# Pooling layer: the transposes of u and of the gated product made by DMAs on 16-bit halves, with the output projection moved behind both u products

## The chip, the cores and the metric

The kernel runs on one core of a Trainium2 chip. The metric is the device time of one execution in microseconds; lower is better. Five engines work side by side: TensorE (PE), VectorE (DVE), ScalarE (ACT), GpSimd (POOL) and SyncE (SP); 16 DMA engines move data between HBM and the on-chip memory SBUF.

## The reference, cut to what matters

All arithmetic is float32. Two layers (retention, then pooling) each add a branch to the residual `h` of 256 tokens by 2048 columns; the change touches only the pooling layer.

```python
def pool_branch(xn, w_in, w_group, scale, w_out):      # xn (1, 256, 2048)
    u, g = jnp.split(xn @ w_in, 2, axis=-1)            # each 4096 wide
    csum = jnp.cumsum(u.astype(jnp.float32), axis=1)
    outs = []
    for gi, w in enumerate((2, 4, 8, 16)):             # 4 groups of 1024 columns
        lo, hi = gi * 1024, (gi + 1) * 1024
        c_g = csum[..., lo:hi]
        c_lag = jnp.pad(c_g, ((0, 0), (w, 0), (0, 0)))[:, :256]
        cnt = jnp.minimum(t + 1, w)[None, :, None]
        outs.append((c_g - c_lag) / cnt - u32[..., lo:hi])
    d = jnp.stack(outs, axis=2)
    mixed = jnp.einsum('bsgc,gce->bsge', d, w_group).reshape(b, s, 4096) * scale
    return (mixed * jax.nn.silu(g)) @ w_out
```

## The kernel before, in words

**Weights and units.** All weights are streamed once, in the order in which they are used, as `stream`: pieces of 1 MB that SP loads into one of four slots of `w_raw`. A piece holds two units. A unit is two blocks of 128 by 512 weights; in the kernel's 552 units every product is done. float32 products are made of three fp32r products: ACT copies the unit to `w_hi` (`split_hi`, line 615, rounded to fp32r), DVE makes `w_lo = w_raw - w_hi` (`split_lo`, line 878), and PE does hi·hi, hi·lo, lo·hi for two blocks and two token tiles, 12 matmuls of 512 columns per unit (`products`, lines 344 to 346). `w_hi` and `w_lo` are rings of `RING = 4` units: `split_hi` of unit u waits until PE has finished unit u - 4.

**Orders.** Each of PE, ACT and DVE runs an order written out by hand: a loop over the units u of a stage, and behind a named unit some other work ("at u = 6"). So a step of ACT "at u" comes behind `split_hi(u)` and in front of `split_hi(u + 1)`, while PE itself is some units behind. The products go to three pairs of PSUM accumulators A, B and C; the transposes on PE go to two further banks, `side`.

**The pooling layer.** It is `group` for g = 0 to 3 (the first written out, the later three a loop) and then `close(1)`. A group of 1024 columns has two column halves of 512. In a later group PE does, in 56 units:

- u 0 to 7: the u product of the first half into A. Behind unit 3 it transposes the gated product `gm` of the second half of the previous group (`m_transposes(n2 - 1, 1)`).
- u 8 to 23: the output projection of the previous group, four column blocks of 4 units into B, C, A, B. Behind unit 13 it transposes `u` of the first half (`u_transposes(n2)`).
- u 24 to 31: the u product of the second half into C. u 32 to 39: the first gate product into A; behind its fourth unit the transposes of `u` of the second half. u 40 to 47: the second gate product into B.
- u 48 to 51 and 52 to 55: the two group products (`w_group`) into C and B; behind unit 53 the transposes of the first half of this group's `gm`.

The first group has no output projection (40 units). One set of transposes is `transpose4` (line 360): 8 float32 transposes of 128 by 128 against the identity `idn`. Around it, ACT copies the product to `u` (`u_part`, line 701), PE transposes it to `side`, ACT copies it to `uT` (`uT_part`, line 709), DVE does six window steps on it, one per unit (`window_step`, lines 1033 to 1047), and ACT and DVE split the result into `dT_hi` and `dT_lo` (lines 715 and 1053). For the gated product, ACT and DVE read `side` and write `oT_hi` and `oT_lo` for the output projection (`m_hi_part`, line 727; `m_lo_part`, line 1075). DVE adds each block of the projection to `h` (line 1145). `close(1)` starts with 4 units of the embedding projection (A, C, A, C; `emb_out` copies them to `emb`), transposes the last half of `gm` behind its unit 2, and goes on with the last output projection.

## Time and profile before

| | us |
|---|---|
| median of 3 runs (1590.47 to 1590.62) | 1590.62 |
| the profiled execution's own time | 1590.46 |
| its span, first to last instruction | 1588.7 |
| outside the span (1590.46 - 1588.7) | 1.8 |
| PE busy | 1576.0 |
| DVE busy | 1020.1 |
| ACT busy | 734.2 |

The profile is one execution. Busy time counts an engine's computing instructions, not its waits and not its issuing of DMAs. TensorE's mean granted clock is 0.998 of full speed.

### The profile page before, as it was taken

How to read it: one execution, taken by the hardware profiler on the slowest of the kernel's cores; microseconds unless marked ns; L12 is line 12 of the kernel's file. 1: busy time of each engine (PE TensorE's matmuls, PEld its weight loads, DVE VectorE, ACT ScalarE, POOL GpSimd, SP SyncE). 2: the span in 40 equal slices, each digit the busy share in tenths (PEclk: the TensorE clock that was granted, in tenths of full speed). 3: DMA queues.
4: the chain of work that ended last, by engine and by line, in shares of the span. 5: the costliest groups of instructions: out<-in, count | busy, mean ns of one | idle time of the engine just before them, and what ended most of it. 6: DMA issues, size and time to landing. Idle time of an engine off the chain costs nothing.

```text
span 1588.7 us, 19508 instructions
## 1 busy us (share of the span) xinstructions
PE 1576.0 (99%) x7162; PEld 1306.5 (82%) x7162; DVE 1020.1 (64%) x1247; ACT 734.2 (46%) x904; POOL 4.6 (0%) x12
## 2 busy tenths in 40 slices
PE   9999999999999999999999999999999999999997
PEld 6888888888888888888888888888888888888885
DVE  6775666667576666657756665756575657566665
ACT  6444444444443434445645544444444444445553
POOL 0000000000000000000000000000000000000000
PEclk9999999999999999999999999999999999999999
DMA  9555455545545454555455454555555555555551
GB/s 375 211 212 178 166 185 185 185 162 208 185 158 186 183 186 173 197 183 183 163 197 194 179 208 172 201 184 189 184 186 189 204 185 185 185 211 186 185 186 79
DMA packets 43446, 300.04 MB, mean 189 GB/s; under 512 B 4832, under 2 KB 4848, under 8 KB 7824
## 3 DMA queue, kind: packets, MB, share of 16 engines
q1 hardware_dynamic: 42272, 295.45, 51.3%
q0 software_dynamic: 704, 3.27, 0.5%
q10 hardware_dynamic: 432, 0.79, 0.2%
q8 instruction: 26, 0.43, 0.1%
q14 instruction: 12, 0.10, 0.0%
HBM read 297.40 MB, written 2.10 MB: 189 GB/s over the span
## 4 chain that ended last, share of the span: by engine, by line
PE 98%; DVE 1%; DMA 0%; ACT 0%; issue 0%; SPq 0%; DVEq 0%; ACTq 0%
PE accB L344 11%; PE accB L346 11%; PE accB L345 11%; PE accA L346 10%; PE accA L344 10%; PE accA L345 10%; PE accC L344 10%; PE accC L346 10%; PE accC L345 10%; PE side L360 2%; DMA w_raw<-in_stream_dram 0%; PE side L399 0%; PE side L398 0%; PE side L397 0%; PE side L388 0%; PE side L389 0%
## 5 line engine op out<-in xcount | busy, mean ns | idle before, releaser
L878 DVE TENSOR_TENSOR w_lo<-w_raw,w_hi 128x1024 fp32r<-128x1024 f32 x551 | 668.9, 1223 | 388.3 <-ACT w_hi L615 384.1
L615 ACT CAST w_hi<-w_raw 128x1024 fp32r<-128x1024 f32 x551 | 579.3, 1055 | 612.5 <-PE accB L346 253.5
L344 PE MATMUL accA<-w_hi,xa_hi 128*128 128x512 f32 x508 | 198.9, 392 | 0.0
L346 PE MATMUL accA<-w_hi,xa_lo 128*128 128x512 f32 x508 | 197.7, 389 | 0.0
L345 PE MATMUL accA<-w_lo,xa_hi 128*128 128x512 f32 x508 | 197.7, 389 | 0.0
L344 PE MATMUL accC<-w_hi,xa_hi 128*128 128x512 f32 x384 | 150.7, 392 | 0.6 <-DVE w_lo L878 0.6
L346 PE MATMUL accC<-w_hi,xa_lo 128*128 128x512 f32 x384 | 149.5, 389 | 0.0
L345 PE MATMUL accC<-w_lo,xa_hi 128*128 128x512 f32 x384 | 149.4, 389 | 0.0
L344 PE MATMUL accB<-w_hi,xa_hi 128*128 128x512 f32 x384 | 149.4, 389 | 0.0
L345 PE MATMUL accB<-w_lo,xa_hi 128*128 128x512 f32 x384 | 149.4, 389 | 0.0
L346 PE MATMUL accB<-w_hi,xa_lo 128*128 128x512 f32 x384 | 149.4, 389 | 0.0
L346 PEld LDWEIGHTS accA<-w_hi,xa_lo 128*128 128x128 f32 x508 | 95.4, 188 | 19.8
L344 PEld LDWEIGHTS accA<-w_hi,xa_hi 128*128 128x128 f32 x508 | 95.4, 188 | 19.3
L345 PEld LDWEIGHTS accA<-w_lo,xa_hi 128*128 128x128 f32 x508 | 95.4, 188 | 19.3
L344 PE MATMUL accB<-w_hi,oT_hi 128*128 128x512 f32 x256 | 99.9, 390 | 0.0
L346 PE MATMUL accB<-w_hi,oT_lo 128*128 128x512 f32 x256 | 99.6, 389 | 0.0
L345 PE MATMUL accB<-w_lo,oT_hi 128*128 128x512 f32 x256 | 99.6, 389 | 0.0
L344 PEld LDWEIGHTS accC<-w_hi,xa_hi 128*128 128x128 f32 x384 | 72.1, 188 | 15.3 <-DVE w_lo L878 1.0
L346 PEld LDWEIGHTS accC<-w_hi,xa_lo 128*128 128x128 f32 x384 | 72.1, 188 | 15.1
L346 PEld LDWEIGHTS accB<-w_hi,xa_lo 128*128 128x128 f32 x384 | 72.1, 188 | 15.0
L345 PEld LDWEIGHTS accB<-w_lo,xa_hi 128*128 128x128 f32 x384 | 72.1, 188 | 14.9
L344 PEld LDWEIGHTS accB<-w_hi,xa_hi 128*128 128x128 f32 x384 | 72.1, 188 | 14.9
(200 smaller groups left out, 2125.0 us busy)
## 6 DMA issues: line engine op xcount, KB each, us to landing
w_raw<-in_stream_dram SPq DMA_DIRECT2D x275, 1024.0 KB, 4.8
h<-in_x_dram SPq DMA_DIRECT2D x4, 512.0 KB, 13.8
xT_raw<-in_xT_dram SPq DMA_DIRECT2D x3, 512.0 KB, 15.4
dec<-in_decay_dram POOLq DMA_DIRECT2D x1, 1024.0 KB, 9.1
fgain<-in_final_gain_dram POOLq DMA_DIRECT2D x1, 1024.0 KB, 5.1
out_dram<-emb SPq DMA_DIRECT2D x1, 1024.0 KB, 3.8
w_raw<-in_stream_dram SPq DMA_DIRECT2D x2, 256.0 KB, 6.4
w_raw<-in_stream_dram SPq DMA_DIRECT2D x1, 512.0 KB, 7.7
```

The source lines that it names most:

```text
L344: pe.matmul(acc[pair][t][:, 0:n], xh, wh, start=first and b == 0, stop=False)
L345: pe.matmul(acc[pair][t][:, 0:n], xh, wl, start=False, stop=False)
L346: mm = pe.matmul(acc[pair][t][:, 0:n], xl, wh, start=False, stop=last and b == UNIT - 1)
L360: mm = pe.transpose(side[j // 2][:, (j % 2) * SEQ + t * P:(j % 2) * SEQ + (t + 1) * P], src(t)[:, tiles + j * P:tiles + (j + 1) * P], idn[:])
L615: act.copy(w_hi[:, r % RING, :], w_raw[:, r // 2, (r % 2) * 1024:(r % 2 + 1) * 1024]).then_inc(hi_ready, 1)
L878: dve.tensor_tensor(w_lo[:, r % RING, :], w_raw[:, r // 2, (r % 2) * 1024:(r % 2 + 1) * 1024], w_hi[:, r % RING, :].bitcast(F32), ALU.subt ...
```

## The change

The float32 tiles `u` and `gm` are transposed without PE. ACT copies a tile of 128 tokens by 512 float32 words, seen as 1024 words of 16 bits, to `halves`, with the lower halves of the words first and the upper halves behind them (`halves_of`, two copies). One unit later ACT issues two DMA transposes of 128 by 1024 16-bit elements (`transpose_halves`). Some units later ACT waits for both to have landed and puts the halves together again, 16 bits beside 16 bits, into `uT` or into `words` (`words_of`, two copies). One such round is a turn: 2 in the first group (u only), 4 in each later one, 14 in all. `halves`, `halvesT` and `words` lie in `emb`, which is not in use until the close. For `gm`, ACT makes `oT_hi` from `words` (`m_words`), and DVE's `m_lo_part` reads `words` where it read `side`. `u_transposes` is gone; `m_transposes` is left only in `close(1)`, for both halves of the last group (behind its units 0 and 2).

In a later group PE's order becomes: u 0 to 7 and 8 to 15 the two u products (A, C), u 16 to 31 the output projection (B, A, C, B), u 32 to 39 and 40 to 47 the gate products (A, C), u 48 to 55 the group products (A, B). The weight stream is put in that order. The turns of ACT in a later group:

| turn | halves | DMA transposes issued | words |
|---|---|---|---|
| `gm`, first half of the previous group | u = 0 | u = 1 | u = 6, with `oT_hi` |
| `gm`, second half of the previous group | u = 6 | u = 7 | u = 13, with `oT_hi` |
| `u`, first half | u = 14 | u = 15 | u = 21 |
| `u`, second half | u = 22 | u = 23 | u = 29 |

In the first group the two turns have halves at u = 11 and 19, the DMAs at 12 and 20, and the words at 18 and 26. The window steps follow the words unit by unit, and the d split comes at six units behind the words. The core of the diff:

```diff
+U_FIRST = (KD_U + 3, 2 * KD_U + 3)
+U_LATER = (2 * KD_U - 2, 3 * KD_U - 2)
+LANDING = 7
+TURNS = 0
...
+        halves = nc.alloc_sbuf_tensor_at("halves", [P, TT, 2, COL], U16, offset=emb0)
+        halvesT = nc.alloc_sbuf_tensor_at("halvesT", [P, 2 * COL // P, SEQ], U16, offset=emb0 + 4096)
+        words = nc.alloc_sbuf_tensor_at("words", [P, COL // P, SEQ], F32, offset=emb0 + 8192)
...
                 if not first:
-                    pe.wait_ge(pg_ready, n2 - 1)
+                    pe.wait_ge(m_ready, n2 - 1)
                 for k in range(KD_U):
                     if first and k % 2 == 0:
                         pe.wait_ge(xT_ready, NC + k // 2 + 1)
                     unit(k, base, "A", xa_hi, xa_lo, k * UNIT, k == 0, k == KD_U - 1, seg)
                     if first and k == 1:
                         h_transposes(2, NC - 1)
-                    if not first and k == 3:
-                        pe.wait_ge(mT_ready, n2 - 1)
-                        m_transposes(n2 - 1, 1)
+                if first:
+                    pe.wait_ge(z_read, NC)
+                else:
+                    pe.wait_ge(pg_ready, n2)
+                for k in range(KD_U):
+                    unit(KD_U + k, base, "C", xa_hi, xa_lo, k * UNIT, k == 0, k == KD_U - 1, seg)
                 if not first:
+                    pe.wait_ge(m_ready, n2)
                     pe.wait_ge(mT_ready, n2)
-                    pe.wait_ge(m_ready, n2)
                     for c in range(NC):
+                        if c == 1:
+                            pe.wait_ge(u_ready, n2 + 1)
                         if c == 2:
-                            pe.wait_ge(u_ready, n2 + 1)
+                            pe.wait_ge(u_ready, n2 + 2)
                         if c == 3:
                             pe.wait_ge(o_read, g * NC + (O_RET + 1))
                         for k in range(PO_U):
-                            unit(KD_U + c * PO_U + k, base, "BCAB"[c], oT_hi, oT_lo, k * UNIT, k == 0,
+                            unit(2 * KD_U + c * PO_U + k, base, "BACB"[c], oT_hi, oT_lo, k * UNIT, k == 0,
                                  k == PO_U - 1, seg)
-                            if c == 1 and k == 1:
-                                u_transposes(n2)
-                    pe.wait_ge(o_read, g * NC + (O_RET + 2))
-                else:
-                    pe.wait_ge(z_read, NC)
-                for k in range(KD_U):
-                    unit(KD_U + o + k, base, "C", xa_hi, xa_lo, k * UNIT, k == 0, k == KD_U - 1, seg)
-                    if first and k == 3:
-                        u_transposes(n2)
                 if first:
                     pe.wait_ge(u_ready, n2 + 1)
                 else:
+                    pe.wait_ge(o_read, g * NC + (O_RET + 2))
+                for k in range(KD_U):
+                    unit(2 * KD_U + o + k, base, "A", xa_hi, xa_lo, k * UNIT, k == 0, k == KD_U - 1, seg)
+                if first:
+                    pe.wait_ge(u_ready, n2 + 2)
+                else:
                     pe.wait_ge(o_read, g * NC + (O_RET + 3))
                 for k in range(KD_U):
-                    unit(2 * KD_U + o + k, base, "A", xa_hi, xa_lo, k * UNIT, k == 0, k == KD_U - 1, seg)
-                    if k == 3:
-                        pe.wait_ge(uT_ready, n2 + 1)
-                        u_transposes(n2 + 1)
+                    unit(3 * KD_U + o + k, base, "C", xa_hi, xa_lo, k * UNIT, k == 0, k == KD_U - 1, seg)
+                pe.wait_ge(d_ready, n2 + 2)
+                pe.wait_ge(pg_ready, n2 + 1)
+                for k in range(PO_U):
+                    unit(4 * KD_U + o + k, base, "A", dT_hi, dT_lo, k * UNIT, k == 0, k == PO_U - 1, seg)
                 if not first:
                     pe.wait_ge(o_read, g * NC + (O_RET + NC))
-                for k in range(KD_U):
-                    unit(3 * KD_U + o + k, base, "B", xa_hi, xa_lo, k * UNIT, k == 0, k == KD_U - 1, seg)
-                pe.wait_ge(d_ready, n2 + 2)
-                pe.wait_ge(u_ready, n2 + 2)
-                for k in range(PO_U):
-                    unit(4 * KD_U + o + k, base, "C", dT_hi, dT_lo, k * UNIT, k == 0, k == PO_U - 1, seg)
-                pe.wait_ge(pg_ready, n2 + 2)
                 for k in range(PO_U):
                     unit(4 * KD_U + PO_U + o + k, base, "B", dT_hi, dT_lo, k * UNIT, k == 0, k == PO_U - 1, seg)
-                    if k == 1:
-                        m_transposes(n2, 0)
...
+                    if c == 0 and layer == 1:
+                        pe.wait_ge(m_ready, 2 * GROUPS - 1)
+                    if c == 1 and layer == 1:
+                        pe.wait_ge(pg_ready, 2 * GROUPS)
                     unit(c, base, "AC"[c % 2], pT_hi[:, layer], pT_lo[:, layer], 0, True, True, seg)
                     if c == 2 and layer == 0:
                         y_transposes(HEADS - 1)
+                    if c == 0 and layer == 1:
+                        m_transposes(2 * GROUPS - 2, 0)
                     if c == 2 and layer == 1:
                         pe.wait_ge(mT_ready, 2 * GROUPS - 1)
                         m_transposes(2 * GROUPS - 1, 1)
...
-            def uT_part(n):
-                act.wait_ge(uT_done, n + 1)
...
+            def u_halves(n):
+                act.wait_ge(u_ready, n + 1)
+                halves_of(u)
+
+            def uT_part(n, turn):
                 if not (isinstance(n, int) and n == 0):
                     act.wait_ge(d_scaled, n)
-                for b in range(2):
-                    cp = act.copy(uT[:, 2 * b:2 * b + 2, :], side[b][:].rearrange("p (k n) -> p k n", n=SEQ))
-                cp.then_inc(uT_ready, 1)
+                words_of(turn, uT)
+
+            def m_halves(n, c):
+                act.wait_ge(m_ready, n + 1)
+                halves_of(gm[:, c, :, :])
+
+            def m_words(n, k0, c, turn):
+                if c:
+                    act.wait_ge(mT_ready, n)
+                words_of(turn, words)
+                act.wait_ge(words_ready, turn * 2 + 2)
+                for j in range(4):
+                    cp = act.activation(oT_hi[:, 4 * c + j, :], words[:, j, :], ACT.Copy, scale=pscale[:, bass.ds(k0 + j, 1)])
+                    if j % 2:
+                        cp.then_inc(mT_hi, 1)
...
+            def halves_of(src):
+
+                for t in range(TT):
+                    act.copy(halves[:, t, :, :], src[:, t, :].bitcast(U16).rearrange("p (n two) -> p two n", two=2)
+                             ).then_inc(halves_ready, 1)
+
+            def transpose_halves():
+
+                for t in range(TT):
+                    act.dma_start_transpose(halvesT[:, :, t * P:(t + 1) * P],
+                                            halves[:, t, :, :].rearrange("p two n -> p (two n)")).then_inc(halvesT_landed, 16)
+
+            def words_of(n, dst):
+
+                act.wait_ge(halvesT_landed, n * (16 * TT) + 16 * TT)
+                for i in range(2):
+                    act.copy(dst[:].bitcast(U16).rearrange("p k (n two) -> p two k n", two=2)[:, i, :, :],
+                             halvesT[:, 4 * i:4 * i + 4, :]).then_inc(words_ready, 1)
...
+                    if not first and u in (1, KD_U - 1):
+                        act.wait_ge(halves_ready, turn * 2 + (2 if u == 1 else 4))
+                    for i, at_u in enumerate(turns):
+                        if u == at_u + 1:
+                            act.wait_ge(halves_ready, turn * 2 + (2 * i + (2 if first else 6)))
                     split_hi(u, base, seg, landings)
+                    if not first and u in (1, KD_U - 1) or u - 1 in turns:
+                        transpose_halves()
...
                     if not first and u == 0:
-                        m_hi_part(n2 - 2, g * KG - KG, 0)
-                    if not first and u == 6:
-                        m_hi_part(n2 - 1, g * KG - KG // 2, 1)
+                        m_halves(n2 - 2, 0)
+                    if not first and u == KD_U - 2:
+                        m_words(n2 - 2, g * KG - KG, 0, turn)
+                        m_halves(n2 - 1, 1)
+                    if not first and u == 2 * KD_U - 3:
+                        m_words(n2 - 1, g * KG - KG // 2, 1, turn + 1)
...
+                    if u == 2 * KD_U + 2:
+                        u_part(n2 + 1, "C", base + 2 * KD_U)
+                    for i, at_u in enumerate(turns):
+                        if u == at_u:
+                            u_halves(n2 + i)
+                        if u == at_u + LANDING:
+                            uT_part(n2 + i, turn + (i if first else i + 2))
+                        if u == at_u + LANDING + WINDOW_STEPS + 1:
+                            d_hi_part(n2 + i, i)
...
-                    if u == 0 and layer == 1:
+                    if u == 3 and layer == 1:
                         m_hi_part(2 * GROUPS - 2, (GROUPS - 1) * KG, 0)
...
-                    if not first and u == 0:
-                        m_lo_part(n2 - 2, g * KG - KG, 0)
                     if not first and u == 2:
                         mix(n2 - 1, 1, "B", base)
-                    if not first and u == 6:
+                    if not first and u == KD_U - 2:
+                        m_lo_part(n2 - 2, g * KG - KG, 0)
+                    if not first and u == 2 * KD_U - 3:
                         m_lo_part(n2 - 1, g * KG - KG // 2, 1)
                     for c in range(NC):
-                        if not first and u == KD_U + PO_U * (c + 1) + 2:
-                            dve.wait_ge(unit_used, base + (KD_U + PO_U * (c + 1)))
+                        if not first and u == 2 * KD_U + PO_U * (c + 1) + 2:
+                            dve.wait_ge(unit_used, base + (2 * KD_U + PO_U * (c + 1)))
                             for t in range(TT):
                                 hc = h[:, t, c * COL:(c + 1) * COL]
-                                ins = dve.tensor_tensor(hc, acc["BCAB"[c]][t][:], hc, ALU.add)
+                                ins = dve.tensor_tensor(hc, acc["BACB"[c]][t][:], hc, ALU.add)
                             ins.then_inc(o_read, 1)
-                    if first and u == early:
-                        dve.wait_ge(inv_landed, 32)
-                    if early <= u <= early + WINDOW_STEPS:
-                        window_step(g, n2, u - early)
-                    if u == early + 6:
-                        d_lo_part(n2, 0)
-                    if 2 * KD_U + o + 6 <= u <= 2 * KD_U + o + 6 + WINDOW_STEPS:
-                        window_step(g, n2 + 1, u - (2 * KD_U + o + 6))
-                    if u == 2 * KD_U + o + 12:
-                        d_lo_part(n2 + 1, 1)
+                    for i, at_u in enumerate(turns):
+                        step = u - at_u - LANDING
+                        if first and i == 0 and step == 0:
+                            dve.wait_ge(inv_landed, 32)
+                        if 0 <= step <= WINDOW_STEPS:
+                            window_step(g, n2 + i, step, turn + (i if first else i + 2))
+                        if step == WINDOW_STEPS + 1:
+                            d_lo_part(n2 + i, i)
...
     for g in range(GROUPS):
         product(pool_in, KD, 0, (g * GDIM, COL))
+        product(pool_in, KD, 0, (g * GDIM + COL, COL))
         if g:
             chunks(pool_out, KG, (g - 1) * KG)
-        product(pool_in, KD, 0, (g * GDIM + COL, COL))
         for c in range(2):
             product(pool_in, KD, 0, (2 * D + g * GDIM + c * COL, COL))
         for c in range(2):
```

## Rows read from the trace of the kernel before

**Rows 1.** The page: the span and the busy times.
```profile
span 1588.7 us, 19508 instructions
PE 1576.0 (99%) x7162; PEld 1306.5 (82%) x7162; DVE 1020.1 (64%) x1247; ACT 734.2 (46%) x904; POOL 4.6 (0%) x12
```

**Rows 2.** The page: the chain that ended last, shares of the span by engine.
```profile
PE 98%; DVE 1%; DMA 0%; ACT 0%; issue 0%; SPq 0%; DVEq 0%; ACTq 0%
```

**Rows 3.** Waits of PE: who waited for whom, us in total, times, longest.
```profile
PE side L588 <- DVE junk L1212: 1.2, 1, 1.2
PE accC L344 <- DVE w_lo L878: 0.6, 1, 0.6
```

**Rows 4.** The chain in order of time: start, us, what; one set a group.
```profile
1063.71 0.87 PE side L360 x8
...
1219.60 0.87 PE side L360 x8
...
1375.49 0.87 PE side L360 x8
```

**Rows 5.** Busy time of one group of 56 units, by engine.
```profile
1063.71:1219.60 155.89, 155.89 (x706) 129.44 (x705) 97.20 (x98) 70.75 (x80) 0.00 (x0) 1.00 0.52 189
```

**Rows 6.** Timeline of PE around one set of transposes: start, us, instruction.
```profile
974.49 0.39 PE L346 MATMUL accA<-w_hi,xa_lo 128*128 128x512 f32 x1
974.72 1.03 PE L360 MATMUL side<-idn,gm 128*128 128x128 f32 x8
...
976.06 0.39 PE L346 MATMUL accA<-w_hi,xa_lo 128*128 128x512 f32 x1
```

**Rows 7.** Groups of instructions by line: count, busy us, mean ns, idle before.
```profile
L615 ACT CAST w_hi<-w_raw 128x1024 fp32r<-128x1024 f32 x551 | 579.3, 1055 | 612.5 <-PE accB L346 253.5 <-PE accA L346 179.4 <-PE accC L346 171.9
...
L1038 DVE SCALAR_TENSOR_TENSOR sums<-sums,wide 128x1024 f32<-128x1024 f32 x24 | 30.7, 1281 | 0.0
...
L627 ACT ACTIVATE junk<-h 128x512 bf16<-128x512 f32 x38 | 23.7, 628 | 17.9 <-DVE h L1022 17.9
...
L709 ACT COPY uT<-side 128x512 f32<-128x512 f32 x16 | 8.6, 590 | 20.2 <-PE side L360 20.2
...
L1145 DVE TENSOR_TENSOR h<-accB,h 128x512 f32<-128x512 f32 x12 | 7.7, 686 | 2.4 <-PE accB L346 2.4
```

**Rows 8.** Timelines of ACT, PE and DVE around one unit's split, PE unhurried.
```profile
964.03 1.06 ACT L615 CAST w_hi<-w_raw 128x1024 fp32r<-128x1024 f32 x1 [1.66 <-PE accB L346]
...
966.56 0.39 PE L344 MATMUL accA<-w_hi,xa_hi 128*128 128x512 f32 x1
...
966.75 1.05 ACT L615 CAST w_hi<-w_raw 128x1024 fp32r<-128x1024 f32 x1 [1.66 <-PE accA L346]
...
967.84 1.23 DVE L878 TENSOR_TENSOR w_lo<-w_raw,w_hi 128x1024 fp32r<-128x1024 f32 x1 [1.38 <-ACT w_hi L615]
```

**Rows 9.** Timeline of ACT around m_hi_part, four activations in one row.
```profile
958.70 1.57 ACT L727 ACTIVATE oT_hi<-side,pscale 128x256 fp32r<-128x256 f32 x4 [2.66 <-PE side L360]
```

**Rows 10.** Timeline of the issuing queues: DMA issues of 256 and 512 KB.
```profile
1.20 0.45 ACTq L823 DMA_DIRECT2D xT_raw<-in_xT_dram  x1
...
12.59 1.93 SPq L278 DMA_DIRECT2D xT_raw<-in_xT_dram  x1
```

**Rows 11.** DMA issues: queue, count, KB each, median us from issue to landing.
```profile
w_raw<-in_stream_dram SPq DMA_DIRECT2D x275, 1024.0 KB, 4.8
...
xT_raw<-in_xT_dram ACTq DMA_DIRECT2D x1, 256.0 KB, 7.0
...
ropes<-in_rope_dram SPq DMA_DIRECT2D x1, 256.0 KB, 15.7
```

**Rows 12.** Waits of ACT for the weight stream: us in total, times, longest.
```profile
ACT w_hi L615 <- DMA w_raw<-in_stream_dram: 6.8, 8, 2.2
```

**Rows 13.** Timeline of ACT in the close, behind PE's transposes.
```profile
1440.75 1.57 ACT L727 ACTIVATE oT_hi<-side,pscale 128x256 fp32r<-128x256 f32 x4 [1.58 <-PE side L360]
1442.20 1.09 ACT L683 COPY emb<-accA 128x512 f32<-128x512 f32 x2
```

More of the change, by code:

```diff
@@ L219, in trunk @@
         st_done = sem("st_done")
+        halves_ready = sem("halves_ready")
+        halvesT_landed = sem("halvesT_landed")
+        words_ready = sem("words_ready")
         pr_whole = sem("pr_whole")
@@ L760, in group @@
                 o = 0 if first else NC * PO_U
-                early = KD_U + (6 if first else PO_U + 4)
                 n2 = g * 2
+                turn = TURNS if first else TURNS - 2 + g * 4
+                turns = U_FIRST if first else U_LATER
                 for u in range(4 * KD_U + 2 * PO_U + o):
+                    if not first and u in (1, KD_U - 1):
[3 more added lines that the diff above has]
+                            act.wait_ge(halves_ready, turn * 2 + (2 * i + (2 if first else 6)))
                     split_hi(u, base, seg, landings)
+                    if not first and u in (1, KD_U - 1) or u - 1 in turns:
+                        transpose_halves()
                     if first and u == 2:
@@ L1023, in add_gated, with window_step @@
                                   ).then_inc(h_ready, 1)
-            def window_step(g, n, i):
+            def window_step(g, n, i, turn):
                 a, b = sums[(i + 1) % 2], sums[i % 2]
@@ L1029, in window_step @@
                 if i == 0:
-                    dve.wait_ge(uT_ready, n + 1)
+                    dve.wait_ge(words_ready, turn * 2 + 2)
                     if not (isinstance(n, int) and n == 0):
@@ L1069, in mix, with m_lo_part @@
                 ins.then_inc(m_ready, 1)
-            def m_lo_part(n, k0, c):
+            def m_lo_part(n, k0, c, last=False):
                 for j in range(4):
@@ L1075, in m_lo_part @@
                     ins = dve.scalar_tensor_tensor(
-                        out=oT_lo[:, 4 * c + j, :], in0=side[j // 2][:, (j % 2) * SEQ:(j % 2 + 1) * SEQ],
+                        out=oT_lo[:, 4 * c + j, :],
+                        in0=side[j // 2][:, (j % 2) * SEQ:(j % 2 + 1) * SEQ] if last else words[:, j, :],
                         scalar=pscale[:, bass.ds(k0 + j, 1)], in1=oT_hi[:, 4 * c + j, :].bitcast(F32),
@@ L1124, in group @@
                 o = 0 if first else NC * PO_U
-                early = KD_U + (6 if first else PO_U + 4)
                 n2 = g * 2
+                turn = TURNS if first else TURNS - 2 + g * 4
+                turns = U_FIRST if first else U_LATER
                 for u in range(4 * KD_U + 2 * PO_U + o):
@@ L1167, in close @@
                     split_lo(u, base, seg)
-                    if u == 0 and layer == 1:
-                        m_lo_part(2 * GROUPS - 2, (GROUPS - 1) * KG, 0)
+                    if u == 3 and layer == 1:
+                        m_lo_part(2 * GROUPS - 2, (GROUPS - 1) * KG, 0, True)
                     if u == 2:
```

27 lines of the change are left out of this document (7 added, 20 removed).

## The prediction

> **What bounds the kernel now.** I read the page's busy times first, then the chain, then who waited for whom, and only then single durations. PE is busy for 1576.0 of 1588.7 us [rows 1], the chain that ended last is 98% PE [rows 2], and PE's own waits in the whole execution are 1.2 and 0.6 us [rows 3]. So time is saved only by taking work from PE's order, and lost only where PE is made to wait. ACT (734.2 us) and DVE (1020.1 us) are far from full [rows 1], but both run in a fixed order in step with PE, so for them a burst at one place counts and not the total.
>
> The unit time comes from ACT's starts, which PE releases: 966.75 - 964.03 = 2.72 us for 12 matmuls, 0.227 each [rows 8]. A later group takes 1219.60 - 1063.71 = 155.89 us, and the next one the same [rows 4]; the stretch is 155.89 us of busy PE, without a gap [rows 5]. 56 units by 2.72 are 152.3; the other 3.6 us are its four sets of transposes.
>
> **What is removed.** Between the matmul at 974.49 and the one at 976.06 lie 1.57 us, in which there would be three steps, 0.68 us, without the transposes [rows 6]. One set so costs PE 0.89 us; 3.6 / 4 gives the same. The chain puts 0.87 us on the eight transposes themselves [rows 4], the rest is the first matmuls behind them. 16 sets exist in the pooling layer, 2 stay in the close, so 14 go: 14 x 0.89 = 12.5 us. This is on the path: PE never waits around them. The matmuls are the same in number and size, so the new order of units saves or costs nothing by itself. A later group should take 152.3 us.
>
> **The accumulators.** The new order must not make PE wait for a pair to be read. Every reader comes two units behind the product's end, and the closest reuse is three: pair B, read at u = 22 of DVE, is needed at u = 28; A, read at 26, at 32; C, read at 30, at 40; the projection waits from u = 16 for `oT`, which DVE has at u = 13. ACT and DVE stand some three units before PE, so each has 8 us or more. Cost 0, covered by these three units; without them it would be one read, 2 x 0.686 us [rows 7], at each change of pair.
>
> **How far ACT may fall behind.** PE starts unit u - 3 at 966.56, ACT starts the split of u at 966.75, DVE ends it at 967.84 + 1.23 = 969.07 [rows 8], and PE needs it at 966.56 + 3 x 2.72 = 974.72. The slack is 5.6 us. ACT's backlog grows at each unit by its work there less 2.72 us. With only a split of 1.06 us [rows 7] it shrinks by 1.66. PE stalls by what the backlog has above 5.6.
>
> **What ACT gets.** A copy of 1024 16-bit elements has no row. The nearest, 1024 float32 elements, takes 1.055 us; two of 512 with a 16-bit output take 2 x 0.628 = 1.26 [rows 7]. If two 16-bit elements went at a time, it would be half of the first, 0.53. I take 1.06, as the engine's time per element is alike in both rows; 1.26 would add 0.2 us per copy, 0.8 at the fullest place. A turn then has halves of 2.1 and words of 2.1 us. For u two copies of 0.590 us go [rows 7]; for `gm` the four activations stay, 1.57 us [rows 9]. ACT's busy time in a group goes from 70.75 [rows 5] to 70.75 + 16 x 1.06 - 4 x 0.59 = 85.3 us, of 152.3.
>
> Let X be the time for which issuing one DMA transpose holds ACT. The bursts of a later group are:
> - u = 0: split and halves, 3.2 us, backlog 0.45. u = 1: split and 2X, backlog 2X - 1.2. PE stalls from X = 3.4 on.
> - u = 6: split, words, activations, halves, 1.06 + 2.1 + 0.2 (a wait for its own copies, estimated) + 1.57 + 2.1 = 7.0, backlog 4.3. u = 7: split and 2X, backlog 2.65 + 2X. PE stalls from X = 1.45 on. This is the tightest place.
> - u = 13 (4.9 us), 14 (3.2), 15: backlog 1.0 + 2X, stalls from X = 2.3.
> - u = 21, 22, 23: backlog 2X - 0.8, stalls from X = 3.2. The two turns of the first group: as u = 0 and 1.
>
> X has no row either. The nearest are plain issues of 256 and 512 KB: 0.45 us on ACT's queue, 1.93 at most on SP's in the crowded start [rows 10]. At 0.45 nothing stalls; at 1.93 the second turn stalls by 2 x (1.93 - 1.45) = 1.0 us, in three groups 2.9 us. I take the nearer one, on ACT's own queue, so 0, and keep 2.9 for the range. Below 0.45 nothing is gained, as PE has no wait left to lose.
>
> **The landing.** Behind the DMAs only ACT waits at first, at the words; but the next splits stand behind it, and DVE's window steps. From issue to words are 13.2 us in the first turn (five units less 0.4), 12.0 in the second, 13.7 and 15.4 in the u turns. Added to the backlogs above, a pair may land up to 14.4, 14.9, about 17.5 and about 19 us behind its issue before PE waits. For 256 KB the rows have 7.0 us on ACT's queue and 15.7 as the worst, in the crowded start [rows 11]. In the steady state 1 MB lands in 4.8 us, so I take under 8 us for the pair: hidden. At 15.7 it costs 1.3 + 0.8 us in each of three groups, 6 us.
>
> The Trainium skill (VectorE: DVE Perf Modes, section "The three transpose paths") speaks against this change: it gives 1309 ns for a 128 by 128 transpose of 16-bit elements by DMA and 390 ns on TensorE. Here eight float32 transposes take 0.87 us, 0.11 each [rows 4]. A turn is 16 such blocks, and by that figure, if they went one by one, 20.9 us; the same skill (Advanced Engine Details and Errata, section "X-Bar Transpose (TRN2)") calls transpose DMAs as fast as regular ones, which would be the 8 us above. No row here shows either.
>
> **The weight stream** gets 14 x 512 KB beside 300 MB. A piece lands in 4.8 us [rows 11], and its slot is asked for about 17.8 us behind its issue (seven units less the split), so 13 us are spare; ACT's waits for it are 6.8 us in all, in 8 waits [rows 12], and PE has none. Cost 0.
>
> **DVE** gets nothing new, but its additions to `h` (2 x 0.686 us) now fall on window steps (1.28 us [rows 7]) at u = 22, 26, 30 and 34. Such a unit is 1.13 + 1.2 + 1.37 = 3.7 us, a plain window unit 2.33. Its backlog stays under some 2.5 us of the 5.6. Cost 0.
>
> **The close.** The set behind unit 0 is new there. ACT makes `oT_hi` from it before it copies the first embedding product out, and PE waits for that copy in front of unit 2. In the same order of ACT now, `oT_hi` starts at 1440.75 and the copies end at 1442.20 + 1.09 = 1443.29 [rows 13], 2.8 us behind the transposes' end at about 1440.47, and PE would be there after 2.8 us. I count 0.2 us.
>
> **The sum**, against the profiled execution: 1590.46 - 12.5 + 0.2 = 1578.2. The median of the runs is 0.16 us above that execution, so 1578.4 us; 0.8% less.
>
> **Rivals.**
> 1. *Partly paid back* (X between 1.45 and 2.9, or copies of 1.26 us, or the second turn landing at 15 to 16 us): the stalls at u = 7 and 15 of the later groups take 1 to 10 us. At X = 2.3 it is 3 x 1.7 = 5.1 us: 1583.5. For it: the fullest unit is 4.3 us behind already. Against: both issue rows are below 2.
> 2. *ACT is held while the DMA transpose runs* (the other side). A transpose can't be one run of bytes; if ACT's queue has to hand it over piece by piece, X grows with its size. The stalls are 3 x [(2X - 2.9) + (2X - 4.6) + (2X - 6.4) + (2X - 6.8)] + 2 x (2X - 6.8), negative terms left out. It decides from X = 2.9, where 3 x (2.9 + 1.2) = 12.3 eat the gain. X = 4 gives 3 x (5.1 + 3.4 + 1.6 + 1.2) + 2.4 = 36 us: 1614. X = 7.0, the landing time of 256 KB [rows 11], gives 3 x (11.1 + 9.4 + 7.6 + 7.2) + 14.4 = 120 us: 1698. Against: plain issues take 0.45 to 1.93 us whatever their size [rows 10].
> 3. *The halves land late* (also slower). It decides from a landing of 16.7 us: 3 x (2.3 + 1.8) = 12.3. At 20 us it is 3 x (5.6 + 5.1 + 2.5 + 1.0) + 2 = 45 us: 1623. For it: 15.7 us occurs for 256 KB [rows 11]. Against: only with many transfers ahead of it. By the Trainium skill's 20.9 us it would be some 55 us more than the forecast.
> 4. *No change* (within 0.2%): stalls that happen to equal the gain, 9 to 15 us.
>
> **Chances.** Forecast 0.48; rival 1 0.13; rival 2 0.21; rival 3 0.12; rival 4 0.06. A measurement of this kernel can tell about 0.2%, 3.2 us, from no change. Faster 0.61, same 0.06, slower 0.33. The likeliest case by itself reaches from 1577.5 to 1584. The range takes in rivals 1 and 4 and the nearer part of 2 and 3: 1576 to 1618, with some 0.18 above it.
>
> **What the profile would show.** PE has 112 transposes fewer; later groups of 152.3 us; ACT some 85 us busy in each; the transposes' issues on ACT's queue below 1.45 us and landed within 13 us; no wait of PE for `w_lo`. Wrong would be: PE waiting for `w_lo` behind u = 7 or 15 (X too small in my sum), ACT waiting for the landing at u = 6 or 13 (rival 3), or waits of ACT for `w_raw` (the stream crowded out).

## The result, and the profile after

| | before | after |
|---|---|---|
| median of 4 runs each, us | 1590.62 | 1579.77 |
| lowest to highest, us | 1590.47 to 1590.75 | 1579.41 to 1579.92 |
| the profiled execution, us | 1590.46 | 1579.41 |
| its span, us | 1588.7 | 1577.6 |

The changed kernel takes 0.9932 of the time, with a 95% interval of 0.9914 to 0.9949: 0.7% faster, 10.9 us. The forecast was 1578.4.

The first lines of the page of the kernel after answer to [rows 1]: PE has 112 instructions and 13.2 us of busy time fewer, ACT 50.9 us more, DVE stays. PE is still busy for 99% of the span.

```profile
span 1577.6 us, 19371 instructions
PE 1562.8 (99%) x7050; PEld 1294.6 (82%) x7050; DVE 1019.1 (65%) x1247; ACT 785.1 (50%) x944; POOL 4.6 (0%) x12
```

The busy time of one later group of 56 units after (columns: the stretch, its length and then PE, PEld, DVE, ACT and POOL) answers to [rows 5]. It is 152.32 us long and PE fills it; the forecast was 152.3. For ACT 85.3 us were forecast, and it has 85.84.

```profile
1109.85:1262.17 152.32, 152.32 (x674) 126.17 (x673) 97.01 (x98) 85.84 (x93) 0.00 (x0) 1.00 0.60 207
```

The waits of PE after (us in total, times, longest) answer to [rows 3]. The waits for `junk` and for `accC` at the start were there before. The one at line 420 belongs to the very first unit, some 8 us into the span. It varies from run to run (0.2 to 1.5 us in the kernels below) and moves nothing behind it: the last transposes of the retention layer start at 857.05 to 857.27 in all these kernels, whatever it is. New in the pooling layer is one wait of 0.8 us for `w_lo`: the sum had none.

```profile
PE side L593 <- DVE junk L1261: 1.2, 1, 1.2
PE accA L420 <- ACT w_hi L656: 1.2, 1, 1.2
PE accA L354 <- DVE w_lo L927: 0.8, 1, 0.8
PE accC L354 <- DVE w_lo L927: 0.7, 1, 0.7
```

It lies in the first group, which I had passed over with the words "as u = 0 and 1". The chain in order of time there (start, us, what) shows ACT from u = 18 to the late split:

```profile
896.22 1.27 ACT u L706 x2
897.49 1.49 ACT uT L753 x2
...
899.79 1.06 ACT w_hi L620
900.84 1.90 ACT halves L740 x2
...
902.76 1.05 ACT w_hi L620
...
904.05 4.17 ACTq L746
...
908.26 1.06 ACT w_hi L620
...
909.34 1.24 DVE w_lo L927
...
910.62 0.50 PE accA L354
```

Two things come together. At u = 18 ACT first copies the second product to `u` and then makes the words of the first turn, so the halves of u = 19 and the issues of u = 20 start from a backlog. And the second of the two issues holds ACT for 4.17 us. The next split starts at 908.26, 5.50 us behind the one before it at 902.76, where 2.72 is the pace. The split of u = 18 had started at 893.55, so at 908.26, three units on, ACT is 908.26 - 893.55 - 8.16 = 6.55 us behind, above the slack of 5.6 by 0.95. The matmul that waited starts 1.23 us behind the one before it (910.62 and 909.39) where 0.23 is the pace, 1.00 late, and the five behind it lose another 0.14: the wait that is listed as 0.84 costs 1.14 us.

The pairs of issues of the first group (two) and of the group behind it (four), from the timeline of ACT (start, us for both issues together):

```profile
878.65 5.60 ACTq L746 DMA_TRANSPOSE halvesT<-halves  x2
902.77 5.45 ACTq L746 DMA_TRANSPOSE halvesT<-halves  x2
957.55 2.79 ACTq L746 DMA_TRANSPOSE halvesT<-halves  x2
978.47 2.77 ACTq L746 DMA_TRANSPOSE halvesT<-halves  x2
998.15 2.62 ACTq L746 DMA_TRANSPOSE halvesT<-halves  x2
1018.03 3.26 ACTq L746 DMA_TRANSPOSE halvesT<-halves  x2
```

So X, which I had taken as 0.45 us, is 1.3 us for one DMA transpose as a rule, and more than that in the two pairs of the first group. SP put out a weight piece just ahead of each of these two:

```profile
878.14 0.33 SPq L294 DMA_DIRECT2D w_raw<-in_stream_dram  x1
...
902.63 0.33 SPq L294 DMA_DIRECT2D w_raw<-in_stream_dram  x1
```

The tightest place of a later group, on ACT's timeline (start, us for all, what, and the idle time ahead with its releaser):

```profile
1123.12 1.05 ACT L620 CAST w_hi<-w_raw 128x1024 fp32r<-128x1024 f32 x1 [1.67 <-PE accA L356]
1124.07 2.57 ACT L753 COPY words<-halvesT 128x1024 uint16<-128x1024 uint16 x2
1126.80 1.71 ACT L728 ACTIVATE oT_hi<-words,pscale 128x256 fp32r<-128x256 f32 x4 [0.15 <-ACT words L753]
1128.41 1.98 ACT L740 COPY halves<-gm 128x1024 uint16<-128x1024 uint16 x2
1130.59 1.05 ACT L620 CAST w_hi<-w_raw 128x1024 fp32r<-128x1024 f32 x1 [0.20 <-ACT halves L740]
1130.60 2.62 ACTq L746 DMA_TRANSPOSE halvesT<-halves  x2
1133.33 2.95 ACT L620 CAST w_hi<-w_raw 128x1024 fp32r<-128x1024 f32 x3 [1.69 <-issue]
```

The split of u = 7 starts at 1130.59, where the pace asks for 1123.12 + 2.72 = 1125.84: a backlog of 4.75 us. The queue begins to issue while the split still runs, so one split and a pair of issues take 1133.33 - 1130.59 = 2.74 us together, and the backlog stays at 4.8 instead of going down. It is below the slack of 5.6 us by 0.8, and PE doesn't wait.

The landing: in the list of DMA issues (count, median us from issue to landing) a DMA transpose of 256 KB has landed after 2.9 us; the longest took 6.8.

```profile
halvesT<-halves ACTq DMA_TRANSPOSE x28, 2.9
```

**Where the time went.** The chain has the transposes of the last set of the retention layer at these times, before (first fence) and after (second), and the first set after the pooling layer's own at 1457.28 and 1446.22.

```profile
857.07 0.87 PE side L360 x8
...
1457.28 0.87 PE side L360 x8
```

```profile
857.21 0.87 PE side L370 x8
...
1446.22 0.87 PE side L370 x8
```

From one to the other are 600.21 us before and 589.01 after: 11.20 us less, which is the gain of 12.46 (14 sets of 0.89) less 1.14 for the wait and less 0.12 for the close and whatever else is small; 0.2 was forecast for the close. The kernel e1 below, which has no such wait, is 1.13 us faster than this profiled execution and has 12.34 us less in the same stretch. The span is 11.1 us shorter.

### The profile page after: what moved, and what is told of

It reads as the page before. It is cut to its first block, busy times and chain, and to the rows that moved or that the text cites. A ratio compares the mean times of both kernels' runs of the same rounds, so it can differ in the third digit from the quotient of the medians.

```text
span 1577.6 us, 19371 instructions
## 1 busy us (share of the span) xinstructions
PE 1562.8 (99%) x7050; PEld 1294.6 (82%) x7050; DVE 1019.1 (65%) x1247; ACT 785.1 (50%) x944; POOL 4.6 (0%) x12
## 4 chain that ended last, share of the span: by engine, by line
PE 97%; ACT 1%; DVE 1%; DMA 0%; ACTq 0%; issue 0%; SPq 0%; DVEq 0%
PE accC L354 11%; PE accC L356 11%; PE accC L355 11%; PE accA L354 11%; PE accA L356 11%; PE accA L355 11%; PE accB L354 9%; PE accB L355 9%; PE accB L356 9%; PE side L370 2%; DMA w_raw<-in_stream_dram 0%; PE side L408 0%; PE side L409 0%; PE side L407 0%; ACTq L746 0%; ACT w_hi L620 0%
## 5 line engine op out<-in xcount | busy, mean ns | idle before, releaser
L354 PE MATMUL accC<-w_hi,xa_hi 128*128 128x512 f32 x512 | 200.4, 391 | 0.7 <-DVE w_lo L927 0.7
L356 PE MATMUL accC<-w_hi,xa_lo 128*128 128x512 f32 x512 | 199.2, 389 | 0.0
L355 PE MATMUL accC<-w_lo,xa_hi 128*128 128x512 f32 x512 | 199.2, 389 | 0.0
L354 PEld LDWEIGHTS accC<-w_hi,xa_hi 128*128 128x128 f32 x512 | 96.2, 188 | 20.5 <-DVE w_lo L927 1.1
L356 PEld LDWEIGHTS accC<-w_hi,xa_lo 128*128 128x128 f32 x512 | 96.1, 188 | 20.0
L355 PEld LDWEIGHTS accC<-w_lo,xa_hi 128*128 128x128 f32 x512 | 96.2, 188 | 19.4
L354 PE MATMUL accB<-w_hi,xa_hi 128*128 128x512 f32 x256 | 99.6, 389 | 0.0
L355 PE MATMUL accB<-w_lo,xa_hi 128*128 128x512 f32 x256 | 99.6, 389 | 0.0
L356 PE MATMUL accB<-w_hi,xa_lo 128*128 128x512 f32 x256 | 99.6, 389 | 0.0
L354 PEld LDWEIGHTS accB<-w_hi,oT_hi 128*128 128x128 f32 x256 | 48.1, 188 | 10.2 <-issue 0.3
```

Source lines behind the costliest of these rows:

```text
L354: pe.matmul(acc[pair][t][:, 0:n], xh, wh, start=first and b == 0, stop=False)
L355: pe.matmul(acc[pair][t][:, 0:n], xh, wl, start=False, stop=False)
L356: mm = pe.matmul(acc[pair][t][:, 0:n], xl, wh, start=False, stop=last and b == UNIT - 1)
```

## The experiments

All times are medians of 4 to 11 runs, against the kernel before on the same chip (1590.6 us in each case). "The changed kernel" is 1579.77 us.

**e1: the turns of the first group one unit earlier.** Theory A: an issue holds ACT long when SP has just put out a weight piece, which it does at every second unit; so units of the other parity are quiet. Theory B: it depends on the group.

```diff
-U_FIRST = (KD_U + 3, 2 * KD_U + 3)
+U_FIRST = (KD_U + 2, 2 * KD_U + 2)
```

> The two turns of the first group one unit earlier: halves at u = 10 and 18, DMA transposes at 11 and 19, words at 17 and 25. Nothing else changes. Theory A (a pair of transposes holds ACT for 5.5 us only when a 1 MB weight piece was issued by SP just ahead of it, which falls on even units): the pairs at u = 11 and 19 hold ACT for 2.6 to 3.3 us, PE's wait of 0.84 us for w_lo is gone, time 1578.4 to 1578.9. Theory B (the first turns of the kernel are slow whatever lies beside them): the pairs stay at 5.5 us; the backlog at u = 19 is 2.75 + 1.06 + 5.5 - 2.72 = 6.6, so PE still waits about 1.0 us, time 1579.5 to 1580.

Measured: 1578.28 us (1578.13 to 1578.41), ratio 0.9922, interval 0.9909 to 0.9936; theory A had 1578.4 to 1578.9, theory B 1579.5 or more. The pairs of the first group, on the timeline of ACT in e1, and the weight piece nearest to the first, from SP's:

```profile
877.83 2.69 ACTq L746 DMA_TRANSPOSE halvesT<-halves  x2
899.53 2.62 ACTq L746 DMA_TRANSPOSE halvesT<-halves  x2
```

```profile
880.29 0.33 SPq L294 DMA_DIRECT2D w_raw<-in_stream_dram  x1
```

They are short now, and PE has no wait for `w_lo` in the pooling layer. 1.5 us are gained over the changed kernel from median to median, and 1.13 from profiled execution to profiled execution; the wait explains 1.14. The profiled execution of the changed kernel is the fastest of its four. The wait differs between executions: in e2 and e8 below, which have the same first group but for e8's single issue, it is 1.5 and 1.3 us, and those two executions took 1580.14 and 1579.83. A longer wait in the other three executions would explain the other 0.4 us of the median; no profile of them shows it.

**e2: the u turns of the later groups one unit later**, so that they fall on units of the other parity, and those for `gm` stay.

```diff
-U_LATER = (2 * KD_U - 2, 3 * KD_U - 2)
+U_LATER = (2 * KD_U - 1, 3 * KD_U - 1)
```

> The two u turns of the later groups one unit later: DMA transposes at u = 16 and 24 in place of 15 and 23, so on even units. Theory A (a weight piece issued just ahead slows the pair): these six pairs hold ACT for 5.3 to 5.6 us each in place of 2.6 to 3.3; the backlog reaches 5.1 to 5.4 of 5.6 us, so the time stays within 1 us of 1579.8. Theory B (only the first turns of the kernel are slow): the six pairs stay at 2.6 to 3.3 us and the time at 1579.8.

Measured: 1579.7 us (1579.63 to 1580.14), ratio 0.9931, interval 0.9917 to 0.9945, as both theories had it. The timeline of ACT in e2, one later group: the two pairs for `gm`, then the two for `u`.

```profile
1110.59 2.90 ACTq L746 DMA_TRANSPOSE halvesT<-halves  x2
1131.32 2.62 ACTq L746 DMA_TRANSPOSE halvesT<-halves  x2
1152.15 5.49 ACTq L746 DMA_TRANSPOSE halvesT<-halves  x2
1173.81 6.25 ACTq L746 DMA_TRANSPOSE halvesT<-halves  x2
```

All six u pairs of the later groups are long (5.5 to 6.3 us, up to 0.7 more than theory A had) and the `gm` pairs short, in the same group. Theory B falls. SP's timeline in e2 has the weight pieces beside them, at 1151.75 and 1173.88:

```profile
1151.75 0.33 SPq L294 DMA_DIRECT2D w_raw<-in_stream_dram  x1
...
1173.88 0.33 SPq L294 DMA_DIRECT2D w_raw<-in_stream_dram  x1
```

In the changed kernel the pieces come 0.51 and 0.14 us ahead of the two long pairs; in e2 0.40 us ahead of three pairs and 0.07 us behind the start of the other three; in e1 the nearest piece comes 2.5 us behind the start of the pair, and holds nothing. PE doesn't wait for the long pairs of the later groups, since the backlog is small at u = 16 and 24. Its one wait in the pooling layer is in the first group, whose second pair takes 6.15 us here in place of 5.45:

```profile
PE accA L354 <- DVE w_lo L927: 1.5, 1, 1.5
```

A piece beside the pair isn't the only thing that lengthens a hold. In the first of the three later groups, and only there, single turns are 1.0 to 2.3 us longer with no piece within 2.3 us of their start: 4.44 us at 1016.17 in e3, 3.89 at 958.25 in e7, and 7.62 for four issues at 958.29 in e4. The same turns of the next two groups take 2.6 to 2.9 us, and 5.4 to 5.5 in e4. No run was made on this.

**e3: the words three units behind the halves instead of seven.** It takes the words of the first turn away from u = 18, and leaves the long pairs.

```diff
-LANDING = 7
+LANDING = 3
```

> LANDING = 3 in place of 7: the words of the u turns come three units behind the halves and not seven; the window steps come earlier with them. In the first group the words so leave u = 18, where u_part stands. If PE's wait of 0.84 us comes from u_part and words at the same unit on top of the long pair, it is gone: backlog at u = 20 is about 0.35 + 1.06 + 5.5 - 2.72 = 4.2, under 5.6, time 1578.4 to 1578.9. If the long pair alone makes the wait, it stays: 1579.8. If the halves needed more than 3 units (8 us less ACT's work) to land, ACT would wait for them at the words in all eight u turns, and the time would be above 1581.

Measured: 1578.82 us (1578.2 to 1579.35), ratio 0.9926, interval 0.9912 to 0.994. In the profiled execution, at 1578.2 us the fastest, the wait for `w_lo` is gone. The other four took 1578.2, 1578.8, 1579.2 and 1579.35; no profile shows what the slower ones waited for. The first pair still takes 5.58 us. The second one, which ACT now reaches 2.5 us sooner, takes 4.00, with a piece put out 0.47 us behind its start. The backlog behind it is 3.7 us; with the 5.45 of the changed kernel it would be 5.2 (an estimate), still below 5.6. So the wait needs both, the long hold and the work piled up at u = 18. A window of two units between issue and words (the DMAs go out one unit behind the halves) is not quite enough for the landing: ACT waits for it at two of the eight u turns, behind the 4.00 us pair and behind the one of 4.44, though PE doesn't.

```profile
ACT uT L753 <- DMA halvesT<-halves: 2.7, 2, 1.6
```

**e4: four DMA transposes of 128 by 512 a turn in place of two of 128 by 1024.** The bytes are the same. If an issue costs by its size, four cost what two did; if it has a price of its own, twice as much.

```diff
                 for t in range(TT):
-                    act.dma_start_transpose(halvesT[:, :, t * P:(t + 1) * P],
-                                            halves[:, t, :, :].rearrange("p two n -> p (two n)")).then_inc(halvesT_landed, 16)
+                    for i in range(2):
+                        act.dma_start_transpose(halvesT[:, 4 * i:4 * i + 4, t * P:(t + 1) * P],
+                                                halves[:, t, i, :]).then_inc(halvesT_landed, 16)
```

> Each turn issues four DMA transposes of 128 by 512 16-bit elements in place of two of 128 by 1024: the same data. If the time for which an issue holds ACT goes by size, a turn holds it for 2.7 us as now, and the time stays at 1579.8. If it is a fixed price of 1.3 us per DMA, a turn holds ACT for 5.4 us: at u = 7 of the later groups the backlog is 2.65 + 5.4 = 8.0, a stall of 2.2 to 2.5 us in three groups, and more in the first group's two turns: 1588 to 1593.

Measured: 1586.34 us (1585.78 to 1588.71), ratio 0.9976, interval 0.9967 to 0.9986. That is below the 1588 to 1593 expected for a fixed price, as the stalls are up to 1.7 us and not 2.2 to 2.5, but far above 1579.8. The issues of e4, by tile (ns, smallest, median and largest), then u = 7 of the later group on ACT's timeline, and the waits of PE:

```profile
L747 ACTq DMA_TRANSPOSE halvesT<-halves x56: 1205/1299/3032, 878.5 to 1333.2; - x56
```

```profile
1133.24 5.19 ACTq L747 DMA_TRANSPOSE halvesT<-halves  x4
```

```profile
PE accC L354 <- DVE w_lo L928: 5.4, 4, 1.7
PE accA L354 <- DVE w_lo L928: 1.7, 1, 1.7
```

Half the size costs the same 1.3 us. Four hold ACT for 5.2 us, 2.6 more than two, and the backlog behind u = 7 is 4.75 + 5.3 - 2.72 = 7.3, above the slack by 1.7: that is the longest wait. Without the one at the start (0.7) there are four waits, 6.4 us; with 0.3 for each restart, as above, they cost 7.6, where the changed kernel has 1.14. The 6.5 between them explain the 6.6 us that e4 lost.

**e5: 2 us more work for ACT at the fullest place.** Three copies of `gm` that nobody reads stand between `m_words` and `m_halves` at u = 6. They take 2.0 us of ACT (2.3 had been expected). It tests the slack of 5.6 us by itself, with X left as it is.

```diff
                         m_words(n2 - 2, g * KG - KG, 0, turn)
+                        act.wait_ge(d_scaled, n2)
+                        act.copy(uT[:], gm[:, 0, :, :].rearrange("p t (k n) -> p (t k) n", n=SEQ))
+                        for t in range(TT):
+                            act.copy(junk[:, t, :], gm[:, 0, t, :])
                         m_halves(n2 - 1, 1)
```

> The changed kernel with 2.3 us more work for ACT at u = 6 of the later groups (three copies of the gated product that nothing reads: 1024 elements to uT, 2 x 512 to junk). Theory (PE stalls by what ACT's backlog has above 5.6 us): in the changed kernel's trace the split of u = 7 starts 4.9 us late and that of u = 8 5.1 us late. With 2.3 us more they come to 7.2 and 7.4, so PE waits for w_lo 1.6 to 1.9 us in each of the three groups, 5 to 6 us in all: 1585 to 1586. Rival (ACT has several us more room there than that): 1579.8 and no wait of PE in these groups.

Measured: 1583.18 us (1583.1 to 1583.3), ratio 0.9954, interval 0.9939 to 0.9969. The timeline of ACT in e5 and PE's waits:

```profile
1124.36 1.05 ACT L620 CAST w_hi<-w_raw 128x1024 fp32r<-128x1024 f32 x1 [1.67 <-PE accA L356]
...
1133.72 1.05 ACT L620 CAST w_hi<-w_raw 128x1024 fp32r<-128x1024 f32 x1
1133.73 2.62 ACTq L746 DMA_TRANSPOSE halvesT<-halves  x2
```

```profile
PE accA L354 <- DVE w_lo L931: 3.6, 4, 0.9
```

The backlog at the split of u = 7 is 1133.72 - 1124.36 - 2.72 = 6.64, above the slack by 1.04. The matmul that waits starts at 1136.08, 1.26 us behind the one before it, so 1.03 late. That is the rule "PE stalls by what the backlog has above 5.6" to 0.1 us. With the restart a group loses 1.2 us, three lose 3.6; the kernel lost 3.4. (The fourth wait of the line is the one of the first group.) The time expected, 1585 to 1586, was missed: it rested on 2.3 us of copies upon a backlog read as 4.9 to 5.1, and both were smaller.

**e6: the kernel before with the new order of units alone**, all 16 sets on PE. Its core, against the kernel before:

```diff
+                for k in range(KD_U):
+                    unit(KD_U + k, base, "C", xa_hi, xa_lo, k * UNIT, k == 0, k == KD_U - 1, seg)
+                    if k == 3:
+                        if not first:
+                            pe.wait_ge(mT_ready, n2)
+                        u_transposes(n2)
...
-                            unit(KD_U + c * PO_U + k, base, "BCAB"[c], oT_hi, oT_lo, k * UNIT, k == 0,
+                            unit(2 * KD_U + c * PO_U + k, base, "BACB"[c], oT_hi, oT_lo, k * UNIT, k == 0,
```

> The kernel before with the new order alone: the output projection behind both u products, accumulator pairs and DVE's additions as in the changed kernel, but all 16 sets of transposes on PE, with their copies out of side. Theory (the order neither saves nor costs, the whole gain is the transposes taken from PE): 1590.1 to 1591.1, PE without waits in the pooling layer. Rival (the order gives part of the gain): below 1589.

Measured: 1590.56 us (1590.48 to 1590.74), ratio 1.0, interval 0.9991 to 1.0009. PE has no wait in the pooling layer. That is the theory's range, and level with the kernel before: the order alone is worth nothing, and the accumulators cost nothing.

**e7: the changed kernel with the eight sets of `u` back on PE**, and only the six of `gm` made by DMAs.

```diff
+            def u_transposes(n):
+                pe.wait_ge(u_ready, n + 1)
+                transpose4(lambda t: u[:, t, :], 0).then_inc(uT_done, 1)
...
-                    if not first and u in (1, KD_U - 1) or u - 1 in turns:
+                    if not first and u in (1, KD_U - 1):
                         transpose_halves()
```

> The changed kernel with the eight transposes of u back on PE; the six sets of the gated product still go by DMA. Theory (0.89 us per set, nothing else): 1590.6 - 6 x 0.89 + 0.2 = 1585.5 us, and no wait of PE in the first group, which has no DMA transposes then. Rival (the sets of u and of the gated product are worth different amounts, as the first group's turns cost a stall): 1584.5 or less, or 1586.5 or more.

Measured: 1585.36 us (1585.26 to 1585.72), ratio 0.9968, interval 0.9955 to 0.998. 1585.5 was expected. Against e6 six sets are gone from PE and 5.2 us, 0.87 each (0.90 if the 0.2 forecast for the close is added); against e1, which has no stall, eight sets are back and 7.1 us, 0.89 each. The price of a set holds from both sides.

**e8: one DMA transpose of 128 by 2048 a turn.** `halvesT` is laid out with the token tile outside, so that one instruction writes it. If an issue has a fixed price, half of it should be saved.

```diff
-                for t in range(TT):
-                    act.dma_start_transpose(halvesT[:, :, t * P:(t + 1) * P],
-                                            halves[:, t, :, :].rearrange("p two n -> p (two n)")).then_inc(halvesT_landed, 16)
+                act.dma_start_transpose(halvesT[:].rearrange("p t k n -> p (t k) n"),
+                                        halves[:].rearrange("p t two n -> p (t two n)")).then_inc(halvesT_landed, 16)
```

> One DMA transpose of 128 by 2048 16-bit elements per turn in place of two of 128 by 1024; turns where they are in the changed kernel. From the run with four small ones: 1.3 us per DMA whatever its size. Then the one holds ACT's queue for 1.3 to 1.5 us, also in the first group, where the first of the two took 1.4 and only the second 4.2; PE's wait of 0.84 us is gone: 1578.2 to 1578.8. Rival (beyond some size the hold goes by size, or a single one also waits for the weight piece issued ahead of it): 2.6 us or more each, 5.5 us in the first group, and 1579.8.

Measured: 1579.8 us (1579.59 to 1579.83), ratio 0.9932, interval 0.9918 to 0.9945, the same as with two. The 1578.2 to 1578.8 expected were missed. The rival's time came true, and its hold in the first group, but not its 2.6 us elsewhere. By tile, and the timeline of PE at its wait:

```profile
L745 ACTq DMA_TRANSPOSE halvesT<-halves x14: 1332/1661/5896, 878.6 to 1323.1; - x14
```

```profile
911.02 0.50 PE L354 MATMUL accA<-w_hi,xa_hi 128*128 128x512 f32 x1 [1.29 <-DVE w_lo L926]
```

Quiet turns hold ACT for 1.3 to 2.1 us in place of 2.6 to 3.3: most of the price is fixed, seen from the other side too, and the double size adds 0.3 us to the median. In the first group it didn't help: the single issue, beside a weight piece, takes 5.31 and 5.90 us, as long as the pair did, and the wait is 1.29 us. The extra time there goes with the piece put out beside it, not with the number of issues.

**e9: e8 with the turns of the first group one unit earlier**, the edit of e1.

> One DMA transpose per turn and the first group's turns on odd units (issues at u = 11 and 19): both edits together. If the holds of 5.3 and 5.9 us with a single DMA come from the weight piece issued ahead, they go to 1.3 to 2.1 us here, PE has no wait for w_lo in the pooling layer, and the time is that of the run with odd turns alone, 1578.0 to 1578.6: PE's order is full, so a shorter hold saves nothing more. If a shorter hold were worth something by itself, the time would be under 1577.8.

Measured: 1578.19 us (1578.1 to 1578.33), ratio 0.9923, interval 0.9909 to 0.9936. Its issues, by tile:

```profile
L745 ACTq DMA_TRANSPOSE halvesT<-halves x14: 1338/1644/2121, 877.7 to 1321.4; - x14
```

No issue is above 2.2 us and PE has no wait in the pooling layer. The time is in the range expected. It is level with e1 (1578.28), and both are 0.1% better than the changed kernel, with no execution in common: once nothing stalls, a shorter issue gives nothing.

## Why the prediction was right, point by point

- **What is removed: right.** 112 instructions fewer, a later group of 152.32 us (forecast 152.3), and 0.87 to 0.89 us a set from e6, e7 and e1.
- **The order and the accumulators: right.** Cost 0 (e6).
- **ACT's copies: right.** I took 1.06 us; the halves take 1.05 and 1.04. The words, written to every second place of 16 bits, take 1.35, 0.3 more. The backlog at u = 7 was 4.75, forecast 4.3.
- **X, the hold of an issue: mis-sized, without effect in the later groups.** Taken as 0.45, measured 1.3. By my own formula, backlog 2.65 + 2X, u = 7 would end at 5.3 of 5.6. With the 4.75 measured in place of the 4.3 forecast it would be 4.75 + 1.06 - 2.72 + 2.7 = 5.8, a stall of 0.2 us in each of three groups. It ends at 4.8, since the first issue starts with the split and not behind it, which my sum didn't have. So the sum was right there for a reason that it lacked, and that part is luck. The place that I named as tightest is, and it held with 0.8 us to spare; e4 and e5 show what lies beyond. Of the bounds (0.45 and 1.93) I took the nearer row, and the truth lay between them.
- **"The two turns of the first group: as u = 0 and 1": wrong, 1.1 us.** The sum left out that u = 18 of the first group has both `u_part` (1.27 us) and the words (2.6 us), with halves and issues right behind; and the pairs there are held 5.5 us by a weight piece. That is nearly all of the miss of 1.2 us between the sum (1578.2) and the profiled execution (1579.41).
- **The landing: right, and far from the bound.** 2.9 us, at most 6.8, of some 12 or more, so rival 3 has nothing in its favour here. The figure isn't fixed: the median is 6.4 us in e2, where eight of the 14 turns have a piece beside them, and 5.1 in e4. The Trainium skill (VectorE: DVE Perf Modes, "The three transpose paths") gives 1309 ns for one 128 by 128 transpose by DMA. By an estimate from it, 8 blocks one by one would be 10.5 us and a turn's 16 blocks 20.9; 2.9 us for the 8 blocks of one transfer don't bear out that they go one by one. The Trainium skill (Advanced Engine Details and Errata, "X-Bar Transpose (TRN2)") also calls transpose DMAs as fast as regular ones. The trace agrees: the two plain 256 KB transfers that store the result at the end, when the weight stream is over, land in 3.5 and 3.6 us.
- **The weight stream: right in its own time, wrong as a neighbour.** A piece still lands in 4.8 us, and ACT's waits for it are 5.6 us in all (6.8 in [rows 12]). I had asked only whether the transposes crowd out the stream, not what a piece does to an issue on another queue.
- **Rival 1** had the right mechanism, a part paid back by the backlog of ACT, at a place that it didn't name, and smaller. **Rival 2**, X growing with the transfer's size until it eats the gain, falls: 512, 1024 and 2048 columns have medians of 1.30, 1.34 and 1.66 us (e4, the changed kernel, e8), so four times the size adds 0.4.
- **DVE: right, cost 0.** A unit with an addition to `h` and a window step takes 3.5 us from start to start (forecast 3.7), a plain window unit 2.33 (forecast 2.33), and no wait of PE comes from them.
- **The close: 0.2 forecast.** The stretch from 857 to the close leaves 0.1 for it and for what else is small; it wasn't measured alone.

Open stays why a weight piece that SP puts out beside an issue on ACT's queue lengthens it. The runs show when (e1, e2, e3, e8, e9) and by how much (3 to 4 us a turn), not by what. Open too are the three longer turns without a piece in the first later group.

## What to carry to other kernels

Here, moving work off the full engine paid its full price as long as the engine that took it over never fell behind by more than the slack; so work out the slack from the trace (here 5.6 us), and add up the bursts at every place, the first pass of a loop that is written out by hand too. Count the issue of a DMA as work of the engine that issues it, 1.3 to 1.7 us here for each DMA transpose of 128 to 512 KB, and issue few and large ones where the engine is short of time. Don't let such an issue follow a large transfer that another queue has just put out; one unit earlier was worth 1.1 to 1.5 us here.

## What the runs showed of the hardware

- A DMA transpose of SBUF to SBUF on ACT's queue holds ACT for 1.2 to 1.3 us at least, for 128, 256 and 512 KB alike; the medians are 1.30, 1.34 and 1.66 us. The plain issue on the same queue in [rows 10] took 0.45.
- With a 1 MB load put out by SP at most 0.5 us ahead of the turn's start, or 0.07 us behind it (three turns of e2), the hold is 3 to 4 us longer (5.4 to 6.3 us for two in place of 2.6 to 3.3, 5.3 to 5.9 us for one in place of 1.3 to 2.1). With the load 0.47 us behind the start (e3) it was 4.0 us.
- ACT's queue starts such an issue while the instruction ahead of it on the engine still runs: 1130.60 beside a split that runs from 1130.59 to 1131.64.
- 256 KB transposed on 16-bit elements land in 2.9 us (median), beside a stream of some 200 GB/s; 512 KB in one transfer in 3.8 us (e8). In e2, where 16 of the 28 go out beside a weight piece, the median is 6.4 us.
- ACT's copy of 1024 16-bit elements takes 1.05 us, the time of 1024 float32 elements, and 1.35 us when it writes to every second 16-bit place.
